# First modulation matrix of a hybrid backbone block: eight row pieces become four column quarters, interleaved with the first two weight units

## The reference

```
cond = silu(c); cond_ctx = silu(c_ctx)
m  = (cond @ w_mod[l] + b_mod[l]) split in 9      # 1024 x 9216 matrix
x  = x + 0.5 * m[2] * swiglu(rmsnorm(x, norm_w[l,0]) * (1 + m[1]) + m[0], ffn1_w13[l], ffn1_w2[l])
swiglu(h, w13, w2) = (silu(gate) * up) @ w2 ;  up, gate = split(h @ w13)      # 2 x 2816 columns
```

## Time and profile before

| | us |
|---|---|
| median of 3 runs | 2603.19 (2602.56 to 2607.49) |
| profiled execution, its own time | 2598.84 |
| its span, first to last instruction | 2597.0 |
| PE busy in the span | 2361.5 (91%) |
| mean granted TensorE clock | 0.958 |

### The profile page before, as it was taken

The page is one execution under the profiler, slowest core; times in us unless marked ns, Lnnn a source line. Parts: engine busy times, 40 slices in busy tenths (PEclk is TensorE's granted clock), DMA queues, the critical chain, the costliest instruction groups (busy, mean ns, idle before and its releaser), DMA issues.

```text
span 2597.0 us, 29283 instructions
## 1 busy us (share of the span) xinstructions
PE 2361.5 (91%) x12273; PEld 1977.4 (76%) x12273; DVE 1365.1 (53%) x1756; ACT 884.0 (34%) x1256; POOL 192.1 (7%) x253
## 2 busy tenths in 40 slices
PE   6999999968987978899999999999998898988998
PEld 4887787847776766778887878877877787878998
DVE  4877524364245453356663258775245645555554
ACT  3322213343234443232222132222134435544442
POOL 0000000000034350000000000000000004320000
PEclk8999999988999998999999999999999998999999
DMA  8656422201321111235553236663222141234663
GB/s 277 194 175 208 136 97 82 66 15 49 99 65 33 56 42 49 98 89 166 169 167 106 98 97 204 186 194 130 97 81 82 57 140 49 65 97 147 170 183 135
DMA packets 298251, 302.05 MB, mean 116 GB/s; under 512 B 7392, under 2 KB 268488, under 8 KB 297096
## 3 DMA queue, kind: packets, MB, share of 16 engines
q1 hardware_dynamic: 297696, 300.00, 36.9%
q10 hardware_dynamic: 424, 0.18, 0.0%
HBM read 299.10 MB, written 1.05 MB: 116 GB/s over the span
## 4 chain that ended last, share of the span: by engine, by line
PE 73%; DVE 13%; ACT 5%; POOL 3%; issue 3%; DMA 2%; SPq 1%; DVEq 0%; POOLq 0%; ACTq 0%
PE PS L1208 22%; PE PS L1209 21%; PE PS L1210 21%; DVE mraw L831 3%; DVE WL L806 2%; DMA mraw<-in_w_mod 2%; PE PS L1564 2%; PE PS L1335 1%; POOL dq L483 1%; PE PS L1525 1%; DVE small L994 1%; PE PS L1301 1%; ACT dq L712 1%; DVE A L1091 1%; POOL dq L498 1%
## 5 line engine op out<-in xcount | busy, mean ns | idle before, releaser
L1208 PE MATMUL PS<-hH,WH 128*128 128x512 f32 (+1 forms) x2096 | 776.7, 371 | 27.5 <-DVE hL L875 15.1
L806 DVE TENSOR_TENSOR WL<-raw,WH 128x1024 fp32r<-128x1024 f32 x420 | 502.5, 1237 | 515.8 <-ACT WH L532 515.3
L1209 PE MATMUL PS<-hL,WH 128*128 128x512 f32 (+1 forms) x2096 | 761.7, 363 | 0.0
L1210 PE MATMUL PS<-hH,WL 128*128 128x512 f32 (+1 forms) x2096 | 760.9, 363 | 0.0
L532 ACT CAST WH<-raw 128x1024 fp32r<-128x1024 f32 x420 | 419.2, 1046 | 418.9 <-PE PS L1210 409.0
L1208 PEld LDWEIGHTS PS<-hH,WH 128*128 128x128 f32 x2096 | 406.7, 194 | 102.2 <-issue 33.2
L1210 PEld LDWEIGHTS PS<-hH,WL 128*128 128x128 f32 x2096 | 405.9, 194 | 60.3
L1209 PEld LDWEIGHTS PS<-hL,WH 128*128 128x128 f32 x2096 | 406.7, 194 | 57.0 <-issue 1.0
L831 DVE SCALAR_TENSOR_TENSOR mraw<-mraw,cst 128x1024 f32<-128x1024 f32 x224 | 274.0, 1278 | 18.1 <-DMA mraw<-in_w_mod 18.1
L1208 PE MATMUL PS<-hidH,WH 128*128 128x512 f32 (+1 forms) x704 | 261.7, 372 | 5.2 <-DVE sg L929 5.2
L1210 PE MATMUL PS<-hidH,WL 128*128 128x512 f32 (+1 forms) x704 | 255.3, 363 | 0.0
(11 more groups left out here) (189 smaller groups left out, 2548.0 us busy)
## 6 DMA issues: line engine op xcount, KB each, us to landing
raw<-in_ffn_w SPq DMA_DIRECT2D x176, 512.0 KB, 5.2
mraw<-in_w_mod SPq DMA_DIRECT2D x128, 512.0 KB, 4.7
raw<-in_w_in SPq DMA_DIRECT2D x54, 1024.0 KB, 5.3
raw<-in_ffn_w SPq DMA_DIRECT2D x44, 1024.0 KB, 4.9
raw<-in_w_branch_attn SPq DMA_DIRECT2D x8, 1024.0 KB, 5.2
raw<-in_w_branch_gla SPq DMA_DIRECT2D x8, 1024.0 KB, 5.3
raw<-in_w_out SPq DMA_DIRECT2D x8, 1024.0 KB, 5.1
mfirst_b<-in_w_mod SPq DMA_DIRECT2D x4, 1024.0 KB, 10.0
```

The costliest lines, as they stand in the source:

```text
L806: nc.vector.tensor_tensor(half(WL, n % 2, e, rows), half(raw, n % 2, e, rows), half(WH, n % 2, e, rows).bitcast(F32), ALU.subtract).then_i ...
L1208: mm(o, wh, ah, start=start, stop=False)
L1209: mm(o, wh, al, start=False, stop=False)
L1210: return mm(o, wl, ah, start=False, stop=stop)
```

## The change

- `w_mod`'s first 2048 columns come in four quarters. Quarter q holds all 1024 rows of columns 256q to 256q+255 of both vectors (two DMAs of 1 MB, 1 KB per row piece), and so everything that tiles 2q and 2q+1 of h need.
- SP issues units 0 and 1 of the weights ahead of the quarters. `x` and `ctx` have a semaphore each, and the transposes, the copies to `xT` and the squares go by pairs of tiles of one half of the tokens. The bias and norm rows are transposed after the sums of squares, no longer first.
- ACT prepares units 0 and 1 before it forms `rstd`.
- PE: `first_rows(q)` is eight matmuls of 512 columns; `first_columns(q)` is four matmuls against a small selection matrix `sel`, which add the four partial sums and transpose at once. They are put between the matmuls of units 0 and 1. DVE works quarter by quarter: copy, bias, `coefA`, two tiles of `sq`, two of `hL`.
- The first two later pieces of `w_mod` may be loaded once quarter 0 has been multiplied.

```diff
-            def load_first(kt):
-                sp.dma_start(first_buf(kt), a["w_mod"][0][kt * P:(kt + 1) * P, 0:MW]).then_inc(mfirst_in[kt], 16)
+            def load_first(q):
+                for v in range(FIRST_MODS):
+                    cols = slice(v * D + q * UW, v * D + (q + 1) * UW)
+                    sp.dma_start(first_buf(q)[:, :, v, :],
+                                 a["w_mod"][0][:, cols].rearrange("(k p) c -> p k c", p=P)).then_inc(mfirst_in[q], 16)
...
-            for kt in range(4):
-                load_first(kt)
             for f in range(2):
                 load_pair(START[("ffn_in", 0)] + f, f, w13_d[0])
-            for kt in range(4, KT):
-                load_first(kt)
+            for q in range(MOD_Q):
+                load_first(q)
...
+                if n == 0:
+                    for q in range(MOD_Q):
+                        first_rows(q)
+                        first_columns(q)
+                        if q == 0:
+                            dve.wait_ge(rstd_done, 1)
+                        xn(2 * q)
+                        xn(2 * q + 1)
+                        lo(2 * q)
+                        lo(2 * q + 1)
+                    return
...
+                if norm == 0:
+                    for kt in range(KT):
+                        pe.wait_ge(h_ready, kt + 1)
+                        if kt == 0:
+                            pe.wait_ge(lo_ready, 2 * n + 2)
+                        first(n, kt)
+                        if kt % 2 == 0 and kt < KT - 2:
+                            first_rows(kt // 2 + 1)
+                        if kt == 0:
+                            pe.wait_ge(lo_ready, 2 * n + 4)
+                        if kt < KT - 2:
+                            second(n + 1, kt)
+                        if kt % 2 == 0 and kt < KT - 2:
+                            first_columns(kt // 2 + 1)
+                    for kt in range(KT - 2, KT):
+                        second(n + 1, kt)
+                    return
...
+            def first_rows(q):
+                pe.wait_ge(mfirst_in[q], 32)
...
+                for e in range(2):
+                    for j in range(MOD_Q):
+                        kt = 2 * j + e
+                        ins = mm(PS[j * MOD_M:(j + 1) * MOD_M, 4 + q % 2, :], cst[:, kt, :],
+                                 first_buf(q)[:, kt, :, :].rearrange("p v c -> p (v c)"),
+                                 start=e == 0, stop=e == 1)
                 ins.then_inc(mod_mm, 1)
+            def first_columns(q):
+                pe.wait_ge(first_row, q + 1)
...
+                for i in range(MOD_Q):
+                    ins = mm(PS[:, 6 + q % 2, 2 * i:2 * i + 2], mrow[:, i * P:(i + 1) * P], sel[:], start=True, stop=True)
+                ins.then_inc(first_t, 1)
```

More of the change, by code:

```diff
@@ L116, in hybrid_backbone @@
         pick = sb("pick", [P, 2, MOD_M])
+        sel = sb("sel", [P, 2])
         ident = sb("ident", [P, P])
@@ L183, in hybrid_backbone @@
         ones_in = sem("ones_in")
-        mfirst_in = [sem(f"mfirst_in{i}") for i in range(KT)]
-        x_in = sem("x_in")
+        mfirst_in = [sem(f"mfirst_in{q}") for q in range(MOD_Q)]
+        x_in = [sem("x_in0"), sem("x_in1")]
+        cond_in = sem("cond_in")
+        sel_ready = sem("sel_ready")
+        first_row = sem("first_row")
+        first_t = sem("first_t")
+        first_mod = sem("first_mod")
+        first_coef = sem("first_coef")
         rows_in = sem("rows_in")
@@ L391, in load_mod @@
                 if p < 2:
[L392 removed]
+                    sp.wait_ge(mod_mm, 1)
                 else:
@@ L549, in norm @@
                 nc.scalar.preload_act_table_set(LN_EXP)
[L550 to L554, removed]
+                if n == 0:
+                    for i in range(KT):
+                        act.wait_ge(x_ready, i + 1)
+                        own = (slice(None), slice(2 * (i % 4), 2 * (i % 4) + 2), slice(i // 4 * S, (i // 4 + 1) * S))
+                        nc.scalar.activation(sq[own], xT[own], ACT.Square).then_inc(sq_done, 1)
+                    prep(0)
+                    prep(1)
+                else:
+                    for kt in range(KT - 2 if j == 2 else 0, KT):
+                        if kt == KT - 1:
+                            prep(second, only=0)
+                        square(n, kt, T)
                     prep(second, only=1)
@@ L807, in prep @@
                                             half(WH, n % 2, e, rows).bitcast(F32), ALU.subtract).then_inc(lo_ready, 1)
-            dve.wait_ge(vec_t, 1)
+            dve.wait_ge(ident_in, 16)
+            nc.vector.tensor_reduce(sel[:], ident[:].rearrange("p (j z) -> p z j", j=MOD_Q)[:, 0:2, :], AX.X, ALU.add).then_inc(sel_ready, 1)
+            for i in range(KT):
+                dve.wait_ge(x_t, i + 1)
+                own = (slice(None), slice(2 * (i % 4), 2 * (i % 4) + 2), slice(i // 4 * S, (i // 4 + 1) * S))
+                nc.vector.tensor_copy(xT[own], PS[:, i, :].rearrange("p (k c) -> p k c", k=2)).then_inc(x_ready, 1)
+            dve.wait_ge(vec_t, 2)
             nc.vector.tensor_copy(bmodT[:, 0:72], PS[:, 5, 0:72])
             nc.vector.tensor_copy(bmodT[:, 72:144], PS[:, 5, 128:200])
-            dve.wait_ge(vec_t, 2)
+            dve.wait_ge(vec_t, 3)
             nc.vector.tensor_copy(nwT[:], PS[:, 6, 0:48])
             nc.vector.tensor_copy(vecT[:], PS[:, 6, 64:88]).then_inc(vec_ready, 1)
-            for kt in range(KT):
-                dve.wait_ge(x_t, kt + 1)
-                nc.vector.tensor_copy(xT[:, kt, :], PS[:, kt, :]).then_inc(x_ready, 1)
             def mod_part(p):
@@ L834, in mod_rows @@
             def mod_rows(v):
[L836 to L841, removed]
-            def mod_columns(v):
[L845 to L851, removed]
+                dve.wait_ge(mod_sum, v - 1)
@@ new lines, in mod_rows @@
+                nc.vector.tensor_copy(mrow[:, 0:D // MOD_Q], PS[:, 4, 0:D // MOD_Q]).then_inc(mod_row, 1)
+            def mod_columns(v):
+                q = KT // MOD_Q
+                dve.wait_ge(mod_t, v - 1)
+                nc.vector.tensor_tensor(mod[:, KT * v:KT * (v + 1), :].rearrange("p (j q) c -> p j q c", j=MOD_Q),
+                                        PS[:, 5, 0:UW].rearrange("p (q j z) -> p j q z", j=MOD_Q, z=MOD_M)[:, :, :, 0:2],
+                                        bmodT[:, KT * v:KT * (v + 1)].rearrange("p (j q) -> p j q", j=MOD_Q).unsqueeze(3)
+                                        .to_broadcast([P, MOD_Q, q, 2]), ALU.add).then_inc(mod_done, 1)
@@ L853, in _ @@
             prep(0)
             prep(1)
-            mod_rows(0)
-            mod_columns(0)
+            def first_rows(q):
+                dve.wait_ge(mod_mm, q + 1)
+                if q:
+                    dve.wait_ge(first_t, q)
+                nc.vector.tensor_copy(mrow[:], PS[:, 4 + q % 2, :]).then_inc(first_row, 1)
+            def first_columns(q):
+                own = slice(2 * q, 2 * q + 2)
+                dve.wait_ge(first_t, q + 1)
+                ins = nc.vector.tensor_tensor(mod[:, 0:FIRST_MODS * KT, :].rearrange("p (v k) c -> p v k c", v=FIRST_MODS)[:, :, own, :],
+                                              PS[:, 6 + q % 2, 0:8].rearrange("p (v k c) -> p v k c", v=FIRST_MODS, k=2),
+                                              bmodT[:, 0:FIRST_MODS * KT].rearrange("p (v k) -> p v k", v=FIRST_MODS)[:, :, own]
+                                              .unsqueeze(3).to_broadcast([P, FIRST_MODS, 2, 2]), ALU.add)
+                ins.then_inc(first_mod, 1)
+                dve.wait_ge(first_mod, q + 1)
+                nc.vector.scalar_tensor_tensor(coefA[:, own, :], mod[:, KT + 2 * q:KT + 2 * q + 2, :], 1.0,
+                                               nwT[:, own].unsqueeze(2).to_broadcast([P, 2, 2]), ALU.add, ALU.mult).then_inc(first_coef, 1)
+                dve.wait_ge(first_coef, q + 1)
@@ L880, in norm, with xn @@
                     prep(next_units(n)[1])
-                dve.wait_ge(rstd_done, n + 1)
-                for kt in range(KT):
+                def xn(kt):
                     for c in range(T // S):
@@ L1295, in mod_total @@
                 pe.wait_ge(mod_acc, 2 * KT * (v - 1))
-                pe.wait_ge(mod_row, v - 1)
                 if v == FIRST_MODS:
                     pe.wait_ge(pick_ready, 1)
+                    pe.wait_ge(first_row, MOD_Q)
+                else:
+                    pe.wait_ge(mod_row, v - FIRST_MODS)
                 for c in range(2):
@@ L1308, in mod_turn @@
             def mod_turn(v):
[L1310 to L1313, removed]
+                pe.wait_ge(mod_row, v - 1)
+                if v > FIRST_MODS:
+                    pe.wait_ge(mod_done, v - FIRST_MODS)
+                for q in range(D // MOD_Q // P):
                     ins = nc.tensor.transpose(PS[:, 5, q * P:(q + 1) * P], mrow[:, q * P:(q + 1) * P], ident[:])
@@ L1318, in _ @@
             pe.wait_ge(ident_in, 16)
[L1319 to L1323, removed]
```

(33 more changed lines are left out.)

51 lines of the change are left out of this document (29 added, 22 removed).

## The result

The changed kernel is slower: median 2615.63 us (2609.93 to 2617.35, 9 runs) against 2602.56 us (2597.08 to 2607.92, 9 runs), a ratio of 1.0047 with an interval of 1.0036 to 1.0058. The forecast was 2600.0. Some 12 us have to be accounted for.

The account below looks back on a forecast made before the run. PE bounds the body, but DVE carries the chain from 65 to 91 us. DVE's 4.82 us of idle time less a 1.6 us later norm gains 3.2 us: 2603.19 - 3.2 = 2600.0 us, range 2596.5 to 2604.0.

Parts of the forecast that it names:

- Removed at the start: 3.2 us; added: nothing on the chain: Sum for the whole kernel: DVE multiplies unit 0 3.2 us earlier, and no new cost lies on the chain.
- Step 3: Loop over quarters in the norm: 8.0 us per quarter, with 1.1 us for a quarter's row matmuls.
- step 2: Start up to the first tile: quarter 0's eight matmuls take 1.9 us; first matmul of unit 0 at 30.7.
- The forecast's own test: End of the norm on DVE: the slower case decides once this comes later than 60.6 us.
- the 4.82 us of idle time: DVE's wait for unit 0's silu before 65.06: it vanishes, less 1.6 us of later norm, gaining 3.2 us.
- Slower than before: Rival, 8%: idle gaps keep the half clock through the norm; DVE ends 9.4 us later, total 2607.8 us.
- Step 4: DVE from norm to mod_total: multiplies unit 0 at 61.8 instead of 65.06; later loads do not decide.
- Sizes of the transfer: Loads at the start: 1 KB pieces at 355 GB/s, 5.9 us a quarter, quarter 0 landing at 23.9.
- The rule of line rate from 512 B on: Rival at the start's loads, 4%: smaller pieces move at the large pieces' rate, everything 3.1 us earlier, 2596.9 us.
- the rival at 18%: At mod_total, 18%: the longer 3.2 us wait drops PE's clock, costing 2.3 us, total 2602.3 us.

Follow-up runs that it names:

- e1: Kernel before plus an unused 8-byte tensor where the change declares sel, shifting every later tensor by 32 bytes: 2612.98 us, ratio 1.0043.
- e9: e7 with a third later piece of w_mod added by DVE before its wait for unit 0's silu: 2595.84 us, ratio 0.9977 to the kernel before.
- e4: Changed kernel with sel kept in unused bytes of epsc's slot, so no tensor moves: 2606.35 us, ratio 1.0018 to the kernel before.
- e6: e4 with PE's quarter steps one place earlier: 2602.56 us, ratio 0.9991 to the kernel before.
- e7: e6 with the first two later pieces of w_mod added by DVE in its idle time: 2598.11 us, ratio 0.9987 to the kernel before.
- e5: e4 with only four of the eight first_rows matmuls in quarters 1 to 3: 2599.47 us, ratio 0.9993 to the kernel before.
- e10: Kernel before with unused bytes so that, of the streamed buffers, hidH alone starts at 32 modulo 64: 2607.79 us, ratio 1.0023.

## Why the prediction was wrong

**What was missing.** The forecast said "Removed at the start: 3.2 us; added: nothing on the chain" and costed the selection matrix as "one DVE instruction before `x` has landed: nothing". Its instruction costs nothing; its declaration costs 11 us (e1: 1.0043). The step was never listed, because the working went through instructions, and the address of a buffer is none. It is the larger part of the result: 1.0043 of shift and 1.0018 of start, which together are 1.0061. That is more than 1.0047 and just above its interval (to 1.0058), but the intervals of the two parts (from 1.0028 and from 1.0008) take it in.

**What was mis-sized.** Step 3 took "1.1" us for a quarter's row matmuls, and step 2 1.9 at the half clock. The rows have x8 records for one old piece of four matmuls (30.56), so eight matmuls are x16: 1.92 us at the full clock, 3.48 at the half. The kernel before shows it in the row of its first two pieces, eight matmuls:

```profile
24.33 1.92 PE L1288 MATMUL PS<-mraw,cst 128*32 128x512 f32 x16
```

The listing of the program's order gave "x8" for instructions, and I read one for the other. It adds 0.8 us to each loop at the full clock, 1.6 us to quarter 0 at the half level, and 1.2 us to quarter 1, which ran at both levels. The loop was 9.1 us, not 8.0; most of the gap is this term. The rest is small: PE waited 0.34 to 0.39 us per loop.

**The chain from it.** First matmul at 33.1 (forecast 30.7), last bias add at 59.8 (53.4), end of the norm at 63.6 (57.4). The forecast's own test was that slower begins "once DVE ends the norm later than 55.83 + 4.82 = 60.6"; it ended 3.0 us past that, and DVE's multiplication was 2.9 us late. The mechanism, the 4.82 us of idle time as the only slack, was right, as was that DVE bounds `mod_total`; e9 confirms it. The rival that ended slower, "Slower than before", put the loss at the start at 4.6 us, and e4 measured 4.7; that is luck, since its cause, a half clock through the norm, did not occur: the clock was full from 38.4 on.

**A smaller miss.** Step 4 said "The later loads do not decide". Yet DVE waited 0.70 us for a piece of `mraw` in the changed kernel (89.27) and 0.80 in e4, just ahead of `mod_total`; in the kernel before it had no such wait. In e4 that is most of the 1.25 us by which `mod_total` was late.

**Right.** Sizes of the transfer: windows of the changed kernel show 347 to 352 GB/s from 20 to 30 us for the 1 KB pieces, against 355 taken, quarter 0 was multiplied from 24.57 (23.9), and no later quarter was waited for. The rule of line rate from 512 B on (the Trainium skill, DMA: Bandwidth & Descriptors, Specifications) did not hold here either: 290 GB/s for the units, 12 to 16 us, and 348 for the quarters. The longer wait at `mod_total` did cost the clock, the rival at 18%: with 3.2 to 3.7 us of idle it fell in the changed kernel, e4, e6 and e7, with 2.86 it stayed in e5, with 0.67 in e9; the price was 2.1 us against 2.3 expected. The length of the wait alone does not decide, though: at the fifth `mod_total` (263.07) the changed kernel's clock fell after 1.97 us of idle, while the kernel before kept it after 1.78 (257.82) and e5 after 2.86.

## What to carry to other kernels

When a change declares a buffer, compare the addresses of all buffers before and after; put a small new tensor into unused bytes of a slot, as e4 did, and check in the trace that the mean of untouched matmuls is what it was. Work that is moved from an engine's idle time into a busy stretch must be counted in that stretch's own records, at both clock levels. And a head start on one engine is worth what the next engine's idle time allows: here e4's loss of 4.7 us became a gain of 6.0 in e9 by two steps, PE's quarter steps one place earlier (e6, 2.3 us under the kernel before, which can't be told from none) and three pieces of DVE's work in its idle gaps.

## What the runs showed of the hardware

Matmuls of 512 columns that stream a float32r buffer started every 227 ns with `hidH` and `hidL` at 0 modulo 64 as they lay before, and every 233 ns with both 32 bytes further. Moving both by 64 gave a period of 10.99 us per 48 matmuls, either one alone at 32 modulo 64 gave 11.09, and both by 32 gave 11.20, against 10.88. Matmuls on `hH` and `hL`, which had not moved, stayed at 227 ns in all of these. The start modulo 64 alone is not the rule: both buffers moved by 64 cost a third of the rise, and `actH` and `actL` moved by 128 (e10) cost all of it, 233 ns in place of 227. Whether the start's relation to another operand's address decides was not tried.
